# A decoder layer on one core: the modulation loaded by thirds, x transposed before it is modulated, and q/k/v and gates in three fp32r passes

## The reference, cut to what matters

```
mod = silu(c) @ w_ada + b_ada              # 9 x 6144; w_ada is 1024 x 6144, 24 MB
sh_a, sc_a, g_a, sh_f, sc_f, g_f = split(mod, 6)
h = rmsnorm(x, ln_mix) * (1 + sc_a) + sh_a
q, k, v, bg, cg, u = split(h @ w_in, 6)    # w_in is 1024 x 3072, 512 columns each
q, k = rope(q), rope(k)
att = differential attention(q, k, v)      # causal for the prompt, paged cache for the samples
conv_out = bg * conv3(cg * u)              # depthwise, causal, width 3
x = x + g_a * (concat[att, conv_out] @ w_out)
h2 = rmsnorm(x, ln_ffn) * (1 + sc_f) + sh_f
x = x + g_f * moe(h2)                      # 32 experts of width 256, two per token
y = rmsnorm(x, ln_final)
```

## Time and profile before

| what | value |
|---|---|
| three runs | 1499.64, 1505.08, 1507.93 us (median 1505.08) |
| the profiled execution | 1510.02 us, its span 1508.2 us |
| mean granted TensorE clock | 0.916 |
| TensorE busy | 1223.8 us (81%) |
| VectorE, ACT, POOL busy | 745.8, 566.9, 281.4 us |
| read from HBM | 220.42 MB |

### The profile page before, as it was taken

How to read it: one execution, slowest core, us unless ns; L and a number is a source line. 1 busy time by engine, 2 the same in 40 slices (tenths; PEclk the granted TensorE clock), 3 DMA queues, 4 the chain that set the end, 5 groups by cost and what they waited for, 6 DMA issues and landing times.

```text
span 1508.2 us, 20187 instructions
## 1 busy us (share of the span) xinstructions
PE 1223.8 (81%) x5817; PEld 833.4 (55%) x5818; DVE 745.8 (49%) x1101; ACT 566.9 (38%) x786; POOL 281.4 (19%) x289
## 2 busy tenths in 40 slices
PE   4879999999998789863667999358999888999920
PEld 1234444456665456542445787247777777777710
DVE  4772222101111787710113454658855746888747
ACT  4540110000000555532333222126754646777633
POOL 0020100010000110000000011023634434444323
PEclk9989999999999899986886999659999999999965
DMA  8991200011100200047777011418856757788545
GB/s 276 377 327 41 87 28 14 28 47 43 42 0 0 86 1 1 1 140 248 223 224 258 32 42 43 174 37 313 304 220 244 276 194 271 304 310 311 206 169 179
DMA packets 84544, 230.86 MB, mean 153 GB/s; under 512 B 16101, under 2 KB 28517, under 8 KB 72165
## 3 DMA queue, kind: packets, MB, share of 16 engines
q1 hardware_dynamic: 70288, 203.80, 38.0%
q0 software_dynamic: 14192, 26.24, 4.9%
HBM read 220.42 MB, written 34.21 MB: 169 GB/s over the span
## 4 chain that ended last, share of the span: by engine, by line
PE 55%; DVE 11%; issue 8%; DMA 8%; SPq 7%; ACT 5%; POOL 2%; DVEq 2%; ACTq 1%; POOLq 0%
PE psum L532 20%; PE psum L585 12%; PE psum L613 11%; DMA xg<-h_scratch,gidx 4%; SPq L407 2%; PE psum L631 2%; DMA wada<-in_w_ada_dram 2%; DVE xgL L1508 2%; PE psum L640 2%; ACT pexp L939 1%; DVEq L333 1%; SPq L416 1%; PE psum L674 1%; SPq L423 1%; PE psum L806 1%
## 5 line engine op out<-in xcount | busy, mean ns | idle before, releaser
L585 PE MATMUL psum<-wqkv,hT 128*128 128x512 f32 (+1 forms) x432 | 188.7, 597 | 0.0
L613 PE MATMUL psum<-hT,wcv 128*128 128x352 f32 x576 | 170.9, 459 | 0.0
L1500 DVE TENSOR_TENSOR wguL<-wgu,wguH 128x2048 fp32r<-128x2048 f32 x64 | 146.7, 2294 | 40.9 <-ACT wguH L1051 40.1
L532 PE MATMUL psum<-wguH,xgH 128*128 128x512 f32 x320 | 131.5, 411 | 32.7 <-DVE xgL L1508 32.7
L613 PEld LDWEIGHTS psum<-hT,wcv 128*128 128x128 f32 x576 | 109.3, 190 | 60.6
L585 PEld LDWEIGHTS psum<-wqkv,hT 128*128 128x128 f32 (+1 forms) x432 | 78.2, 183 | 104.0 <-issue 104.0
L1051 ACT CAST wguH<-wgu 128x2048 fp32r<-128x2048 f32 x64 | 120.4, 1910 | 24.4 <-issue 14.6
L532 PE MATMUL psum<-wguH,xgL 128*128 128x512 f32 x320 | 127.4, 398 | 0.0
L532 PE MATMUL psum<-wguL,xgH 128*128 128x512 f32 x320 | 127.0, 397 | 0.0
L1568 POOL TENSOR_SCALAR small<-small 128x1 f32<-128x1 f32 (+3 forms) x36 | 24.1, 670 | 473.5 <-ACT ajunk L1028 173.8
L720 PE MATMUL psum<-cst,kseq 128*128 128x128 f32 x256 | 48.8, 342 | 56.6 <-DMA kseq<-in_cache_k_dram 28.1
(11 more groups left out here) (269 smaller groups left out, 2236.6 us busy)
## 6 DMA issues: line engine op xcount, KB each, us to landing
wgu<-in_w_gate_dram SPq DMA_DIRECT2D x32, 1024.0 KB, 4.9
wgu<-in_w_up_dram SPq DMA_DIRECT2D x32, 1024.0 KB, 7.5
wdn<-in_w_down_dram SPq DMA_DIRECT2D x32, 1024.0 KB, 7.0
wada<-in_w_ada_dram SPq DMA_DIRECT2D x24, 1024.0 KB, 8.2
kseq<-in_cache_k_dram SPq DMA_DIRECT2D x64, 256.0 KB, 2.9
vseq<-in_cache_v_dram SPq DMA_DIRECT2D x64, 256.0 KB
yg<-y_scratch SPq DMA_DIRECT2D x16, 512.0 KB, 5.1
wqkv<-in_w_in_dram SPq DMA_DIRECT2D x1, 6144.0 KB, 24.1
```

The lines of the kernel that those rows point to most:

```text
L532: ins = mm(out, r32(x(c)), r32(w(c)), start=(begin and c == 0 and k == 0), stop=(end and c == chunks - 1 and k == 2))
L585: last = mm(psum[0:n, 2 + j, :], hT[:, c, P * t:P * t + n], wqkv[:, c, AW * j:AW * j + AW], start=(c == 0), stop=(c == DC - 1))
L613: last = mm(psum[:, 3 * (n % 2) + j, 0:TB], wcv[i % 2][:, c, j, :], hT[:, c, TB * tb:TB * tb + TB], start=(c == 0), stop=(c == DC - 1))
L1500: TT(r32(wguL[slot][:, g, :, :]), wgu[slot][:, g, :, :], wguH[slot][:, g, :, :], ALU.subtract).then_inc(S["wguL_done"], 1)
```

## The change

It rewrites all that comes ahead of attention; what follows keeps its instructions.

- Modulation: w_ada is multiplied in plain f32, not split. Four products of 512 columns each go to four groups of 32 PSUM partitions (`ada_products`), with silu(c) padded to 32 columns as weights, for one chunk of 128 rows of w_ada (1 MB) at a time. The first third (columns 0 to 2047: shift_a and scale_a) is done at the start, 8 chunks through 4 buffers. The other two thirds, 16 chunks through 2 buffers, are multiplied between the slots of the gates, one after every second slot (`CHUNK_AT`), and POOL stores them to DRAM (`store_mod`); the rows of the first third stay on the chip, transposed to columns (`modT`).
- Tokens: all 9 tiles of x are loaded at the start, scaled by the inverse root, transposed and copied into hT before the modulation is there (banks 0 to 3). Then VectorE modulates hT in place by columns, in five pieces of up to 256 tokens (`modulate`), and splits it into hTH (ACT) and hTL (VectorE).
- q/k/v: three blocks of 512 columns of w_in, the weight loop outside: all 9 tiles for q, then for k, then for v, each 24 passes (8 chunks x 3). The blocks are loaded and split ahead, through two places. PSUM is a ring of three banks; the transposes of tile m - 1 follow tile m. VectorE's first rotation stands behind all five pieces and the lambda chain.
- Gates: 12 units (cg, u, bg for each i) of 36 slots, each 24 passes of 352 columns; weights of 128 x 1024 through three places; two sets of three banks. cg and bg are taken from PSUM three banks at a time, bg straight into the multiply; cu holds one i.
- mixA and mixC swap places; a few semaphores are shared; the wait for the last tap copies (ncT) moves from attention into the gates.

The core of the diff:

```diff
+            for c in range(4):
+                load_ada(c)                      # wada[c % 4] <- w_ada_v[:, c, 0:2 * D]
...
+            for c in range(4, DC):
+                sp.wait_ge(W["ada_ps"], c - 3)
+                load_ada(c)
...
+            load_block(0)
...
+            sp.wait_ge(W["ada_ps"], DC)
+            load_block(1)
...
+            sp.wait_ge(W["qkv_ps"], NT)
+            load_block(2)
...
+            for slot in range(36):
+                u, tb = divmod(slot, 3)
+                if slot in CHUNK_AT and CHUNK_AT[slot] + 2 < 2 * DC:
+                    sp.wait_ge(W["adb_ps"], CHUNK_AT[slot] + 1)
+                    load_ada2(CHUNK_AT[slot] + 2)
+                if tb == 2 and u + 3 < 12:
+                    sp.wait_ge(W["cv_ps"], slot + 1)
+                    load_unit(u + 3)
...
+            for t in range(NT):                  # pe: x before the modulation
+                n = rows(t)
+                pe.wait_ge(W["xn_done"], t + 1)
+                if t >= 2:
+                    pe.wait_ge(W["xT_sb"], t - 1)
+                for c in range(DC):
+                    last = tr(psum[:, 2 * (t % 2) + c // 4, P * (c % 4):P * (c % 4) + n], xn[t % 2][0:n, P * c:P * c + P], ident[0:n, 0:n])
+                last.then_inc(S["xT_ps"], 1)
+            def ada_products(bank_, c, weights, done):
+                for j in range(4):
+                    last = mm(psum[32 * j:32 * j + 32, bank_, :], condT[:, c, :], weights[:, 512 * j:512 * j + 512], start=(c == 0), stop=(c == DC - 1))
+                last.then_inc(done, 1)
...
+            for b in range(3):
+                for t in range(NT):
+                    m, n = NT * b + t, rows(t)
+                    if m >= 3:
+                        if m - 3 < 2 * NT:
+                            pe.wait_ge(W["rope_done"], m - 2)
+                        else:
+                            pe.wait_ge(W["v_done"], m - 2 - 2 * NT)
+                    if b == 0:
+                        pe.wait_ge(W["hL_done"], t // 2 + 1)
+                    for u in range(2):
+                        if t == 0:
+                            pe.wait_ge(W["winL_done"], 2 * b + u + 1)
+                        last = three_passes(psum[0:n, m % 3, :], lambda c: hTH[:, 4 * u + c, P * t:P * t + n], lambda c: hTL[:, 4 * u + c, P * t:P * t + n],
+                                            lambda c: wblkH[b][:, 4 * u + c, :], lambda c: wblkL[b][:, 4 * u + c, :],
+                                            4, begin=(u == 0), end=(u == 1))
+                    last.then_inc(S["qkv_ps"], 1)
+                    if 1 <= m <= 2 * NT:
+                        row_transposes(m - 1)    # waits rope_done m
...
+                last = three_passes(psum[:, 3 * (u % 2) + tb, 0:TB], lambda c: wcvH[u % 3][:, c, :], lambda c: wcvL[u % 3][:, c, :],
+                                    lambda c: hTH[:, c, TB * tb:TB * tb + TB], lambda c: hTL[:, c, TB * tb:TB * tb + TB], DC)
+                last.then_inc(S["cv_ps"], 1)
+                if slot in CHUNK_AT:
+                    n = CHUNK_AT[slot]
...
+                    ada_products(7, n % DC, wada2[n % 2], S["adb_ps"])
...
+            for t in range(NT):                  # act
+                if t + 3 < NT:
+                    squares(t + 3)
+                copy_xT(t)
...
+            lead_of_h(0)
+            lead_of_block(0, 0)
+            lead_of_block(0, 1)
+            for p in range(1, len(PIECES)):
+                lead_of_h(p)
...
+            def modulate(p):                     # dve
+                a, n = PIECES[p]
+                if p < 4:
+                    for c in range(DC):
+                        h = hT[:, c, a:a + n]
+                        last = TS(h, h, modT[:, 1, c, 0:1], modT[:, 0, c, 0:1], ALU.mult, ALU.add)
...
+            modulate(0)
+            rest_of_h(0)
+            rest_of_block(0, 0)
+            modulate(1)
+            rest_of_block(0, 1)
+            rest_of_h(1)
+            for p in range(2, len(PIECES)):
+                modulate(p)
+                rest_of_h(p)
...
+            for r in range(2 * NT):
+                b, t = divmod(r, NT)
+                if t in (5, 6):
+                    rest_of_block(b + 1, t - 5)
+                rotate(r)
```

More of the change, by code:

```diff
@@ L157, in build @@
[L157 to L165, removed]
@@ L175, in build @@
[L175 to L180, removed]
+        wcv = [at(f"wcv{i}", O_R0 + 8 * K * i, [P, DC, P]) for i in range(3)]
@@ L379, in _ @@
[L379 to L399, removed]
@@ new lines, in lead_of_h, with lead_of_unit @@
+            def lead_of_h(p):
+                a, n = PIECES[p]
+                act.wait_ge(W["h_done"], p + 1)
+                nc.scalar.copy(r32(hTH[:, :, a:a + n]), hT[:, :, a:a + n]).then_inc(S["hH_done"], 1)
+            def lead_of_unit(u):
+                act.wait_ge(W[f"win_in{u % 3}"], 16 * (u // 3 + 1) + BLK_IN[u % 3])
+                nc.scalar.copy(r32(wcvH[u % 3][:, :, :]), wcv[u % 3][:, :, :]).then_inc(S["winH_done"], 1)
+            for t in range(3):
+                squares(t)
@@ new lines, in three_banks @@
+            def three_banks(u):
+                return psum[:, 3 * (u % 2):3 * (u % 2) + 3, 0:TB]
+            for u in range(12):
+                if u >= 1 and u + 2 < 12:
+                    lead_of_unit(u + 2)
+                if u % 3 == 0:
+                    act.wait_ge(W["cv_ps"], 3 * u + 3)
+                    if u:
+                        act.wait_ge(W["cu_done"], u)
+                    nc.scalar.copy(cg_sb[:, :].rearrange("p (b n) -> p b n", b=3), three_banks(u)).then_inc(S["cg_done"], 1)
@@ new lines, in modulate @@
+            def modulate(p):
+                a, n = PIECES[p]
+                if p < 4:
+                    for c in range(DC):
+                        h = hT[:, c, a:a + n]
+                        last = TS(h, h, modT[:, 1, c, 0:1], modT[:, 0, c, 0:1], ALU.mult, ALU.add)
+                    last.then_inc(S["h_done"], 1)
+                else:
+                    h = hT[:, :, a:a + n].rearrange("p c (s l) -> p c s l", s=NSEQ)
+                    gain, shift = (modT[:, k, :, 1:NSEQ + 1].unsqueeze(3).to_broadcast([P, DC, NSEQ, LNEW]) for k in (1, 0))
+                    link(TT(h, h, gain, ALU.mult))
+                    TT(h, h, shift, ALU.add).then_inc(S["h_done"], 1)
@@ new lines, in _ @@
+            dve.wait_ge(W["modT_ps"], 1)
+            dve.wait_ge(W["xT_sb"], NT)
+            columns = psum[:, 5, :].rearrange("p (q k j r) -> p k j q r", q=4, k=2, j=2)
+            for k in (1, 0):
+                for j in range(2):
+                    last = nc.vector.tensor_copy(modT[:, k, 4 * j:4 * j + 4, :], columns[:, k, j, :, 0:NSEQ + 1])
+                last.then_inc(S["modT_sb"], 1)
+            dve.wait_ge(W["modT_sb"], 2)
+            modulate(0)
+            rest_of_h(0)
+            rest_of_block(0, 0)
```

562 lines of the change are left out of this document (286 added, 276 removed).

## The result

The changed kernel takes 1406.74 us, the median of 4 runs (1402.08 to 1410.36), against 1506.51 for 4 runs of the kernel before (1499.64 to 1511.75): a ratio of 0.9336, 95% interval 0.9305 to 0.9367. Predicted were 1407 us. The profiled execution took 1407.08 us, its span 1405.2.

What follows compares the result with a forecast made beforehand. Before 111 us w_ada's load sets the pace, then TensorE's f32 matmuls to 484. First row maximum at 392.0, 98.9 us earlier: 1510.0 - 98.9 = 1411.1, on the runs' scale 1406.2, said as 1407; range 1388 to 1440.

Steps and rivals of the forecast that it cites:

- The chunk-by-chunk front: Ahead of the projection: w_ada's first third loads through four buffers, chunks in at 42 us, modulation columns ready at 48.
- VectorE's serial queue: Modulation pieces, remainders, lambda chain and first rotation in program order: 34.4 us, so the first rotation ends at 82.4.
- The stall before the third tile: In q/k/v, TensorE stands still about 12 us after tile 1, waiting for VectorE's rotation behind all pieces.
- The clock after the stall: First q/k/v passes after TensorE's pause run at a lowered clock: 2.9 us added.
- q/k/v: Projection stage from first rotation to gates: 25 tiles of 24 passes at 0.2273 us plus transposes, 148.8 us, ending at 231.2.
- The gates: Gate stage: 864 passes at 0.163 us, 140.8, plus 17.6 for 16 modulation chunks; splits and loads hidden; ends at 389.6.
- The handover: From the last gate pass to attention's first row maximum: 2.4 us, maximum at 392.0, the rest carried over unchanged.
- (a): Gates: a pass doesn't shrink with its columns, 864 x 0.227, +55, 1462 us; chance 0.07.
- (c): q/k/v and gates: passes reach f32's small extra of 2.9 ns at both widths, 18 less, 1389 us; chance 0.05.
- (b): Modulation chunks among the gates: column groups don't overlap beside full-width passes, +37, 1444 us; chance 0.04.
- (d): Front: loads on one queue and VectorE's serial pieces hold the first rotation to 110 instead of 82, +28, 1435; chance 0.11.
- (e): q/k/v and gates: TensorE idling in every tile keeps the clock at half, slower than before; chance 0.03.

Runs made afterwards that it cites:

- The early rotations: Changed kernel with VectorE doing rotations 0 and 1 in the waits for the casts of pieces 2 and 3: 1395.88 us, ratio 0.926.
- the tiles with f32: Changed kernel with q/k/v in one plain f32 product of the leading parts per chunk, remainders made but not multiplied: 1440.56 us, ratio 0.9561.
- eight buffers: Changed kernel with the eight chunks of w_ada's first third going to eight buffers instead of four: 1407.58 us, for 1408.16 of the changed kernel beside it.

## Why the prediction held, step by step

- **The chunk-by-chunk front.** TensorE was through with x at 27.3 us (26 to 28), chunk 4 cost it a wait of 2.5 us, and the chunks then landed every 2.5 us, at 419 GB/s from 35 to 40 us; the modulation columns were there at 45.2 us, not 48. Of the 2.8 us, 1.1 lie in the loads (the last chunk at 40.9 for 42; four chunks took 9.9 us, which would be 11.0 at the 381 GB/s of the earlier trace rows), and the larger part, 1.7, in the short steps behind them, 4.3 us for the estimated 6.
- **VectorE's serial queue.** A piece took 2.59 to 2.68 us, not 2.25: a 128x256 tensor_scalar has a pitch of 0.32 us and not 0.28. (A straight line through the two sizes of the earlier trace rows gives 0.35; the 0.28 was too low for its own rows.) The whole list took 35.4 us for 34.4, and with the 2.8 us gained in front the first rotation ended at 80.58 (82.4). The stall before the third tile is 11.89 us (about 12), ended by the rotation, as said. The early rotations show that it cost just that and the cold passes behind it.
- **The clock after the stall.** 24 passes took 6.91 us instead of 5.56: 1.35, not 2.9. The term was also read from the wrong place: the 13.82 us of the earlier trace rows are a piece of the chain between two instructions of VectorE, not a pause of TensorE, which was busy in 14.99 of the 20 us. By the timeline of the kernel before, TensorE's own pause there was 3.10 us:

```profile
839.27 0.79 PE L532 MATMUL psum<-woutH,mixH 128*128 128x512 f32 x1 [3.10 <-DVE mixL L1347]
```

- **q/k/v.** 149.8 us from the rotation to the gates, for 148.8. Four terms were off and cancel in part: a pass takes 232.1 ns, not 227.3 (+2.9 us for 600 of them; 232 is what the earlier trace rows had shown for other passes of 512 columns), the clock 1.5 less, the first group of transposes 1.1 and not 0.5, and the end 0.7 (229.75 to 230.41) and not 1.6. The later groups of transposes cost 0.42 a tile (0.44).
- **The gates.** 157.0 us, for 158.4. A pass of 352 columns takes 158.8 ns, between the ends 149.6 and 227 and 4 under the 163 taken: -3.6 us for 864. A chunk takes 1.21 us (8.83 less 48 x 0.1588), not 1.1: the product itself 0.99, and the first step on either side of it 0.10 longer than the others. It was 0.90 in the front, four chunks in a row. The splits and the 16 MB are hidden, as said: passes and chunks alone make 156.6 of the 157.0 us.
- **The handover.** 2.0 us from the last pass to the first maximum (2.4), and 1015.8 us after it (1017.3). The sum of the steps, 1411.1 on the profile's scale, came out at 1407.1, so the steps together were 4.0 us too long. That 1407 and 1406.74 lie 0.3 us apart is luck: 4.9 us were taken off for the runs' scale, since the profiled execution of the kernel before lay that much over its median, and the changed kernel's lies 0.3 over its own.
- **The rivals.** (a) and (c) fall with 158.8 and 232.1 ns. (b) falls with the 1.21 us of a chunk. (d) falls with the first rotation at 80.6. (e) falls with a clock of 0.98 and 1.00 in the windows above. The rule of the Trainium skill behind (c) ("TensorE: Matmul & The Clock Gate", Back-to-back issue gap) would give 149 and 216 ns for these widths; the trace doesn't agree for fp32r, and the measurement decides. For f32 it agrees within 1%: the tiles with f32 repeat 858 ns for 512 columns (6.87 us for eight), 214.5 for each of the four times that the columns stream.

The one thing that the prediction had as a price and not as an opportunity is the stall: its length was forecast well, and moving two rotations up in VectorE's order takes it away.

## What to carry to other kernels

Price a matmul form by the steps between starts, at the width that it will have, and write both ends down where a width isn't in the trace: here the estimate from the columns was within 3%, and below an estimated 250 columns the weight load is the floor (the 112 ns measured at 176 columns, over the 0.45 ns a column of the two wider passes). A load ahead of the first dependent work was paid here by its bytes over the rate of the queue, so load first what the next stage needs, and the rest beside a stage that computes. When an engine's serial list opens a stage, look where it waits for another engine, and put into those waits what the next engine in line will stop for; before giving a load more buffers, look not only whether its queue is idle but also which loads come forward with it and share the queue.

## What the runs showed of the hardware

- The extra time of an fp32r pass was not the same at the two widths: 18.8 ns over 512 columns at 2.4 GHz, 12.1 over 352. The whole pass is 0.453 and 0.451 ns a column. The prediction took the extra as a constant. The output projection's passes of 512 columns take 227, 5 less than those of q/k/v; why isn't known.
- A chunk of four f32 products in 32-column groups costs 0.90 us in a row and 1.21 alone between full-width passes; 0.2 of it are the two changes from one kind to the other.
- The step of matmuls with few columns follows the columns of the weights: at a granted clock of 0.50 and 36 columns in f32, 213 ns with weights of 128 columns and 60 with 32; at 1.00 and 176 columns in fp32r, 111.6 with 128.
- The DMA engines held 419 to 423 GB/s over stretches of 5 to 20 us while chunks of w_ada (1 MB in rows of 2048 columns) landed. It was 304 where the weight block and smaller loads came in between (eight buffers, 35 to 40 us), and the 381 of the earlier trace rows is from a stretch with other loads and with w_ada in rows of 512 columns; which of the two made that one slower isn't shown.
